# Top-2 expert selection in two token halves, and a first gather table built straight from the token numbers

## The reference

```python
hn = rms_norm(x, norm_ffn[l])
x = x + hier_moe(hn, ...)
# hier_moe, cut
g_idx = jnp.argmax(xt @ w_rg + b_rg, axis=-1)               # 1 group of 4
e_sel = e_logits of that group                              # 8 experts in it
top_v, top_i = lax.top_k(e_sel, 2)                          # 2 experts of the 8
top_w = jax.nn.softmax(top_v, axis=-1) * g_w
h = silu(xt @ w_gate[e]) * (xt @ w_up[e])
out = out + (h * combine[e]) @ w_down[e]
```

## Time and profile before

| | |
|---|---|
| median of 3 runs | 605.76 us (605.17 to 606.72) |
| the profiled execution | 605.26 us, its span 603.5 us |
| PE busy | 577.0 us (96%) |
| DVE busy | 260.3 us (43%) |
| ACT busy | 215.0 us (36%) |
| memory read, written | 147.31 MB, 15.75 MB |
| granted clock of TensorE | 0.999 of 2.4 GHz |

### The profile page before, as it was taken

How to read it: one execution, slowest core, us unless ns; L and a number is a source line. 1 busy time by engine, 2 the same in 40 slices (tenths; PEclk the granted TensorE clock), 3 DMA queues, 4 the chain that set the end, 5 groups by cost and what they waited for, 6 DMA issues and landing times.

```text
span 603.5 us, 8714 instructions
## 1 busy us (share of the span) xinstructions
PE 577.0 (96%) x3442; PEld 437.3 (72%) x3445; DVE 260.3 (43%) x584; ACT 215.0 (36%) x437; POOL 60.3 (10%) x104
## 2 busy tenths in 40 slices
PE   7999999999999999999999998999999999887795
PEld 4978989888788888888888874766666666543452
DVE  4646677645445765533472375212111211103255
ACT  6634566555786522422152241011111111111114
POOL 3110000001000001100000012012211121112001
PEclk9999999999999999999999999999999999999999
DMA  8365130712231222197789677999999999999995
GB/s 296 92 205 177 59 111 5 287 62 71 71 104 46 61 70 71 38 344 280 287 315 406 248 259 273 389 414 423 424 421 423 424 427 419 424 425 424 424 421 208
DMA packets 59291, 155.78 MB, mean 258 GB/s; under 512 B 8284, under 2 KB 38388, under 8 KB 47600
## 3 DMA queue, kind: packets, MB, share of 16 engines
q1 hardware_dynamic: 54512, 145.74, 63.2%
q0 software_dynamic: 4720, 9.45, 4.1%
q10 hardware_dynamic: 16, 0.00, 0.0%
HBM read 147.31 MB, written 15.75 MB: 270 GB/s over the span
## 4 chain that ended last, share of the span: by engine, by line
PE 79%; DMA 11%; DVE 3%; SPq 3%; ACT 1%; issue 1%; POOL 1%; DVEq 0%; POOLq 0%; ACTq 0%
PE mid_rows L810 17%; PE last_rows L810 16%; PE bank L1247 12%; DMA slot2b<-expert_w_up 9%; PE bank L810 7%; PE bank L803 5%; PE mid_rows L1267 5%; SPq L554 3%; PE bank L1321 2%; PE mid_rows L945 2%; PE last_rows L868 2%; PE mid_rows L1340 1%; DMA w<-w_in 1%; PE bank L1347 1%; PE mid_rows L868 1%; PE bank L923 1%
## 5 line engine op out<-in xcount | busy, mean ns | idle before, releaser
L1247 PE MATMUL bank<-slots,xgT 128*64 128x256 f32 x544 | 73.0, 381 | 4.5 <-DMA slot2b<-expert_w_up 1.9
L1910 DVE TENSOR_TENSOR w_low<-w,w_high 128x1024 fp32r<-128x1024 f32 x32 | 39.2, 1225 | 78.6 <-ACT w_high L1524 78.6
L1247 PEld LDWEIGHTS bank<-slots,xgT 128*64 128x64 f32 x544 | 49.2, 137 | 22.2 <-issue 4.0
L1524 ACT ACTIVATE w_high<-w 128x1024 fp32r<-128x1024 f32 x32 | 33.7, 1054 | 48.6 <-PE last_rows L810 48.6
L2265 DVE TENSOR_SCALAR y<-mid_rows,slot_weights 128x512 f32<-128x512 f32 x14 | 10.5, 751 | 88.4 <-PE mid_rows L1267 88.4
L1699 ACT ACTIVATE y<-mid_rows,slot_weights 128x512 f32<-128x512 f32 x14 | 9.6, 687 | 84.5 <-PE mid_rows L1267 56.4
L1247 PE MATMUL bank<-slot2b,xgT 128*64 128x256 f32 x208 | 32.9, 381 | 0.0
L1267 PE MATMUL mid_rows<-slots,hT 128*64 128x512 f32 x112 | 29.1, 594 | 2.7 <-issue 2.7
L1693 ACT ACTIVATE h_silu<-bank 128x256 f32<-128x256 f32 x14 | 5.4, 384 | 66.3 <-PE bank L1247 66.3
L810 PE MATMUL mid_rows<-x_high,w_high 128*128 128x512 f32 x72 | 28.7, 399 | 0.0
L810 PE MATMUL mid_rows<-x_high,w_low 128*128 128x512 f32 x72 | 28.2, 391 | 0.0
(11 more groups left out here) (430 smaller groups left out, 1391.5 us busy)
## 6 DMA issues: line engine op xcount, KB each, us to landing
slots<-expert_w_up SPq DMA_DIRECT2D x18, 1024.0 KB, 23.9
slots<-expert_w_gate SPq DMA_DIRECT2D x17, 1024.0 KB, 12.4
slots<-expert_w_down SPq DMA_DIRECT2D x15, 1024.0 KB, 23.9
slot2b<-expert_w_gate SPq DMA_DIRECT2D x9, 1024.0 KB, 16.9
w<-w_in SPq DMA_DIRECT2D x16, 512.0 KB, 3.6
slot2b<-expert_w_up SPq DMA_DIRECT2D x8, 1024.0 KB, 27.5
slot2a<-expert_w_down SPq DMA_DIRECT2D x6, 1024.0 KB, 21.4
w<-w_in SPq DMA_DIRECT2D x7, 840.0 KB, 4.5
```

The costliest lines, as they stand in the source:

```text
L1247: ins = mm(bank[2][e * SLOTS:(e + 1) * SLOTS, m * FE:(m + 1) * FE], xgT[:, c, e * SLOTS:(e + 1) * SLOTS], weights(own, m, e, c * FE, (c + ...
L1524: A(wh2[:, u % 2, :], raw2[:, u % 2, :], ACT.Copy).then_inc(s["hi_done"], 1)
L1910: V.tensor_tensor(wl2[:, u % 2, :], raw2[:, u % 2, :], wh2[:, u % 2, :].bitcast(F32), ALU.subtract).then_inc(s["lo_done"], 1)
```

## The change

Five things are done together.

1. The selection is cut into functions that take a range of tiles. Tiles 0 and 1 (`lo`) are selected, up to the key of their second choice, before DVE waits for the logits of tiles 2 and 3; tiles 2 and 3 (`hi`) follow, with the last two steps of `lo` between theirs. For this ACT takes two of DVE's four copies of turned tiles, and `token_major(0, 2, 1)` goes between the two halves of the last tile's turn.
2. Pair 0 gets a table of its own. `hot` is compared with the whole number `place` (its constant `first_slots` has the offset of the number in it), and the product has 2 columns, the tokens' numbers. DVE makes column 0 of `gtab` from it, and GpSimd gathers. The old table with its 16 columns is made after that, for pairs 1 to 15.
3. SP issues part 20 only after GpSimd has issued the first gather (`pool_step`).
4. Pair 0's gathered rows are turned into four places in four banks, and copied out in quarters, two by ACT and two by DVE.
5. `keep_busy` counts go from 22, 11, 17 to 14, 5, 8, 5.

```diff
@@ SP
             sp.wait_ge(s["hT_done"], 2 * NT)
+            sp.wait_ge(s["pool_step"], 1)
             load_part(20)
@@ GpSimd
             pool.wait_ge(s["gcolm_done"], 1)
             first_gather(0)
+            pool.sem_inc(s["pool_step"], 1)
             pool.wait_ge(s["xt_done"], 2)
+            pool.wait_ge(s["gcolm_done"], 2)
             first_gather(1)
@@ TensorE
             for k in range(2 * NT):
                 pe.wait_ge(s["hot_done"], k + 1)
+                ins = mm(bank[3][:, TABLE][:, 0:2], hot[:, k, :], by_pair[:, k, 0:2], start=(k == 0),
+                         stop=(k == 2 * NT - 1), skip_group_check=True)
+            ins.then_inc(s["first_done"], 1)
+            keep_busy(8)
+            for k in range(2 * NT):
+                pe.wait_ge(s["hot_done"], 2 * NT + k + 1)
                 ins = mm(bank[3][:, TABLE][:, 0:PAIRS], hot[:, k, :], by_pair[:, k, :], ...)
             ins.then_inc(s["first_done"], 1)
-            keep_busy(17)
+            keep_busy(5)
+            def turn_first():
+                pe.wait_ge(s["gathered0"], 16)
+                xv = xg[0].rearrange("p (q c) -> p c q", c=KC)
+                for c in range(KC):
+                    at = bank[(0, 1, 5, 4)[c // 2]][:, (c % 2 + (2 if c >= 6 else 0)) * P:]
+                    ins = tr(at[:, 0:P], xv[:, c, :])
+                    if c == 1:
+                        ins.then_inc(s["first_done"], 1)
+                    if c % 4 == 3:
+                        ins.then_inc(s["xt_done"], 1)
@@ ScalarE
+            act.wait_ge(s["hT_done"], 4)
+            A(hnT[:, 4:8, P:2 * P], bank[TURNED[1][1]][:, :]..., ACT.Copy).then_inc(s["hnT_outA"], 1)
@@ VectorE
+            g_, e_ = maxima_of(lo)
...
+            l_ = second_key(lo, e_)
+
+            router_out(2, 4, 6)
+            dve.wait_ge(s["rl_out"], 2)
+            g_, e_ = maxima_of(hi)
...
+            for e in range(2):
+                V.tensor_scalar(first_slots[:, e * SLOTS:(e + 1) * SLOTS]..., K["iota"][...]...,
+                                UNIT + e * (SEQ - SLOTS), None, ALU.add)
+            V.tensor_copy(by_pair[:, :, 0:2], bc(K["tokval"], 2))
...
             link(V.tensor_reduce(place[:].rearrange("p (k t) -> p k t", k=2), sel[:], AX, ALU.add))
+            for w in range(2):
+                ks = slice(w * NT, (w + 1) * NT)
+                V.tensor_tensor(hot[:, ks, :], first_slots.unsqueeze(1).to_broadcast([P, NT, P]), bc(place[:, ks], P),
+                                ALU.is_equal).then_inc(s["hot_done"], NT)
...
+            dve.wait_ge(s["first_done"], 1)
+            link(V.tensor_scalar(ztab[:, 0:1], bank[3][:, TABLE][:, 0:1], float(NOWHERE), None, ALU.add))
+            V.tensor_scalar(gtab[:, 0:1], ztab[:, 0:1], 1, None, ALU.logical_shift_right).then_inc(s["gcolm_done"], 1)
```

More of the change, by code:

```diff
@@ L1176, in _ @@
             turn_hn(3)
-            token_major(0, 2, 1)
             route(2, 3)
@@ L1188, in _ @@
                start=False, stop=False, skip_group_check=True)
-            keep_busy(22)
+            keep_busy(14)
             pe.wait_ge(s["selb_done"], 1)
@@ L1241, in gate_or_up @@
                 for c in range(KC):
[L1242 to L1245, removed]
+                    if m == 0 and c % 2 == 0 and halved:
+                        pe.wait_ge(s[("xgt_outA", "xgt_outD")[c // 2 % 2]], c // 4 + 1)
+                    if m == 0 and c == 0 and not halved:
+                        pe.wait_ge(s["xgt_outA"], n + 2)
+                    if m == 0 and c == KC // 2 and not halved:
+                        pe.wait_ge(s["xgt_outD"], n + 2)
                     for e in range(2):
@@ L2172, in _ @@
[L2172 to L2184, removed]
+            def maxima_of(ts):
+                return step(V.tensor_reduce(gmax[:, ts], g_lg[:, ts], AX, ALU.max)), step(V.tensor_reduce(v1[:, ts], e_lg[:, ts], AX, ALU.max))
+            def at_maximum(ts, g_, e_):
+                after(g_)
+                g_ = step(V.tensor_tensor(g_hot[:, ts], g_lg[:, ts], bc(gmax[:, ts], NG), ALU.is_equal))
+                after(e_)
+                return g_, step(V.tensor_tensor(one1[:, ts], e_lg[:, ts], bc(v1[:, ts], NE), ALU.is_equal))
@@ new lines, in keyed, with best_key @@
+            def keyed(ts, g_, e_):
+                after(g_)
+                g_ = step(V.tensor_tensor(g_hot[:, ts], g_hot[:, ts], keys4[:, ts], ALU.mult))
+                after(e_)
+                return g_, step(V.tensor_tensor(one1[:, ts], one1[:, ts], keys8[:, ts], ALU.mult))
+            def best_key(ts, g_, e_):
+                after(g_)
+                g_ = step(V.tensor_reduce(gkey[:, ts], g_hot[:, ts], AX, ALU.max))
+                after(e_)
+                return g_, step(V.tensor_reduce(ekey[:, ts], one1[:, ts], AX, ALU.max))
@@ new lines, in first_choice, with without_first @@
+            def first_choice(ts, g_, e_):
+                after(g_)
+                g_ = step(V.tensor_tensor(g_hot[:, ts], g_hot[:, ts], bc(gkey[:, ts], NG), ALU.is_equal))
+                after(e_)
+                return g_, step(V.tensor_tensor(one1[:, ts], one1[:, ts], bc(ekey[:, ts], NE), ALU.is_equal))
+            def without_first(ts, e_):
+                after(e_)
+                return step(V.scalar_tensor_tensor(out=second[:, ts], in0=one1[:, ts], scalar=-3e38, in1=e_lg[:, ts], op0=ALU.mult,
+                                                   op1=ALU.add))
@@ new lines, in second_maximum, with at_second @@
+            def second_maximum(ts, g_, e_):
+                after(e_)
+                e_ = step(V.tensor_reduce(v2[:, ts], second[:, ts], AX, ALU.max))
+                after(g_)
+                step(V.tensor_tensor(one1[:, ts], one1[:, ts], bc(g_hot[:, ts], NE), ALU.mult))
+                return e_
+            def at_second(ts, e_):
+                after(e_)
+                e_ = step(V.tensor_tensor(one2[:, ts], second[:, ts], bc(v2[:, ts], NE), ALU.is_equal))
+                return e_, step(V.tensor_tensor(gap[:, ts], v2[:, ts], v1[:, ts], ALU.subtract))
@@ new lines, in second_keyed, with second_key, second_choice @@
+            def second_keyed(ts, e_, d_):
+                after(e_)
+                e_ = step(V.tensor_tensor(one2[:, ts], one2[:, ts], keys8[:, ts], ALU.mult))
+                after(d_)
+                return e_, step(V.tensor_tensor(gap[:, ts], gap[:, ts], g_hot[:, ts], ALU.mult))
+            def second_key(ts, e_):
+                after(e_)
+                return step(V.tensor_reduce(ekey[:, ts], one2[:, ts], AX, ALU.max))
+            def second_choice(ts, e_):
+                after(e_)
+                return step(V.tensor_tensor(one2[:, ts], one2[:, ts], bc(ekey[:, ts], NE), ALU.is_equal))
@@ new lines, in second_in_group @@
+            def second_in_group(ts, e_):
+                after(e_)
+                return step(V.tensor_tensor(one2[:, ts], one2[:, ts], bc(g_hot[:, ts], NE), ALU.mult))
+            lo, hi = slice(0, 2), slice(2, 4)
+            g_, e_ = maxima_of(lo)
+            g_, e_ = at_maximum(lo, g_, e_)
+            g_, e_ = keyed(lo, g_, e_)
+            g_, e_ = best_key(lo, g_, e_)
+            g_, e_ = first_choice(lo, g_, e_)
+            e_ = without_first(lo, e_)
+            e_ = second_maximum(lo, g_, e_)
```

97 lines of the change are left out of this document (53 added, 44 removed).

## The result

The change made the kernel slower by 0.2%: 606.54 us against 605.16 us (medians of 20 runs each), ratio 1.0021, interval 1.0014 to 1.0028. That is 1.3 us. The forecast was 1.2 us the other way, 604.5 us.

A forecast was written before the change was run, and what follows sets the result against it. The bound was taken to be the weight stream, which loses 6.7 us before it is full. TensorE gains 1.3 us, the stream 1.2 to 2.2; 605.76 - 1.2 = 604.56, rounded 604.5 us, range 602.9 to 606.6.

The forecast's parts named there:

- What bounds the kernel: Weight stream: full from 392 to 590 us, so only the 6.7 us it loses before then can move the end.
- The tail hangs on the stream: End of the kernel: weights, then rows for the final sum, shift with the stream; no size of its own.
- Selection in halves: DVE's selection of tiles: 0.6 us less, less 0.1 us for later last logits; net gain 0.5 us.
- Table from the whole number: DVE between `place` and `hot`: ten instructions leave the path, gain 1.3 us; the gather would start 1.8 us earlier.
- What the gather meets, part 20: First gather: 0.2 us lost beside DVE's second table, 0.6 us to part 20, issued at 370.4 once GpSimd lets go.
- the term of 0.6 us: First gather: slowed 0.6 us by part 20, which comes when it is past its first half; bounds 0 and 1.8.
- The 0.2 us for DVE's instructions beside the gather: GpSimd's part of the first gather: held 0.2 us by DVE's two `hot` instructions; bounds 0 and 1.3 us.
- `keep_busy`: TensorE's useless products: 14 instead of 21 take 3.1 us, out of the way of an earlier `selb`; no gain counted.
- if TensorE's clock falls in the shorter `keep_busy`: Sign of being wrong: TensorE's clock falls there and the turns get slower; no size given.
- Turning in quarters: Landing of the gather to first gate product: copies run beside the turns, gain 0.3 us, bounds 0 and 0.4.
- TensorE's lead and the sum: Start of pair 0: 1.3 us earlier on TensorE; with the stream's 1.2 to 2.2, a gain of 1.2 us taken.
- Rival C: Gather meets the stream: lands after 8.1 us instead of 3.48, pair 0 2.5 us later; up to 608.3 us; chance 0.10.

The follow-up runs named there:

- before_hold: Kernel before, with part 20 held until GpSimd's issue of the first gather and 27 instead of 17 useless products; 608.74 us, ratio 1.0048 to the kernel before.
- before_fill7: Kernel before, with 7 instead of 17 useless products behind the table; 607.69 us, ratio 1.0039 to the kernel before.
- nohold: Changed kernel without SP's wait for pool_step ahead of part 20; 605.01 us, ratio 0.9993 to the kernel before.
- before_fill22: Kernel before, with 22 instead of 17 useless products behind the table; 605.25 us, ratio 0.9997 to the kernel before.
- fill_all: Changed kernel with all four counts of useless products raised (16, 7, 9, 15 for 14, 5, 8, 5); 604.53 us, ratio 0.9988 to the kernel before.
- fill15: Changed kernel with 15 instead of 5 useless products behind the second table; 605.05 us, ratio 0.9993 to the kernel before.
- no_first_table: nohold_fill_all with pair 0's own table taken out and counts 16, 11 and 23; 604.44 us, ratio 0.9987 to the kernel before.
- late20: Changed kernel with part 20 issued only once the first gather has landed, ahead of part 22; 605.5 us, ratio 1.0005 to the kernel before.
- hold_table2: Changed kernel with part 20 held until the second table's product, and counts 16, 7, 9, 9; 605.14 us, ratio 0.999 to the kernel before.
- nohold_fill_all: The best version: changed kernel without the hold of part 20, counts 16, 7, 9, 11; 603.4 us, ratio 0.9966 to the kernel before.

## Why the prediction was wrong

*What bounds the kernel*: right. The stream's rate over 367 to 390 us goes with the ratios to about 0.2% (before_hold 261 GB/s, the changed kernel 269, before_fill7 271, nohold 294, before 300, before_fill22 302, fill_all 306, fill15 and no_first_table 308, the best 324), but for late20 (306 GB/s) and hold_table2 (326 GB/s): there TensorE's wait for the second gather comes behind, and the stream falls to 419 GB/s in 390 to 480 us, 423 in the best version. That is 0.9 us given back later. What it leaves out is TensorE's clock near the end, which added 1.4 us to the traced execution of before_fill7 and some 2.6 us to that of before_hold; there the chain runs over TensorE's products, not over a transfer. The prediction had no term for it ("The tail hangs on the stream").

*Selection in halves*: right, 0.77 us against 0.6 (3.59 for 4.36). The last logits did not come later, where I had taken 0.1. *Table from the whole number*: from the end of `selb` to the start of `hot` are 1.49 us (363.26 to 364.75), and were 2.94 (364.46 to 367.40); 1.3 us of these 1.45 had been forecast. From `hot` to `gtab` it is 2.26 and was 2.20. So `gtab` came 2.59 us earlier, 0.4 of it not from the change, where 1.8 were forecast.

*What the gather meets, part 20*: the step that failed first. "It goes out at 368.9 + 0.2 + 1.19 + 0.1 = 370.4" had it behind GpSimd's work on the gather; it went out at 367.95, 0.13 us ahead of the start of it. Its data and the gather's therefore ran together from the start, and the term of 0.6 us was 1.9 (5.36 for 3.48). That is the upper bound that I had named, 1.8, taken from the second gather of the earlier trace rows. before_hold shows it by itself: a gather of 5.28 us, a stream later by 1.83 us, and a kernel slower by 0.5%, part of which arises in the tail. The 0.2 us for DVE's instructions beside the gather were nothing: GpSimd's part stayed at 1.20 us, and in late20 the gather was as fast as alone.

*`keep_busy`*: the step that failed worst, since it has no term in the sum at all. I asked whether the fillers stand in the way, and not what they cover. The prediction names the falling clock only among the signs of being wrong ("if TensorE's clock falls in the shorter `keep_busy`"). From the counts it could have been worked out: the old set kept TensorE busy until 1.16 us before the turns, and the new one ends 2.28 us before them. The runs give its price: ten products more in the new kernel win 1.5 to 1.7 us, and ten fewer in the old one cost 2.4 us, 1.04 of them at the head. The Trainium skill, TensorE: Matmul & The Clock Gate, section Why this matters for your kernels, treats idle gaps of TensorE as what takes its clock back to 1.2 GHz. The rows agree in kind (0.50 after the gaps of 2.28 and 3.21 us, 1.00 in fill15 and fill_all, where they were filled). They differ in size: the gaps that the Trainium skill warns of are longer than the 2.28 us here and the 1.20 us in nohold, and the measurement decides.

*Turning in quarters*: right at full clock. From landing to the first gate product it took 1.1 us (372.69 to 373.77 in nohold_fill_all), 1.49 before.

*TensorE's lead and the sum*: "TensorE thus starts pair 0 earlier by 1.8 - 0.2 - 0.6 + 0.3 = 1.3 us". Its first gate product came 0.4 us earlier (375.29 for 375.70) and the half gate 0.5 us later. Rival C had the right sign and the right place, but its price (a gather of 8.1 us) was not what happened; the gather took 1.9 us longer, and the clock did the rest. Undoing one cause gave 0.28% (nohold) or 0.33% (fill_all), both together 0.55%: they add up, as far as the intervals tell.

Open: how much of the clock's fall hangs on each gap. In the trace of nohold it fell behind 1.20 us of standing still, in no_first_table it did not, and in late20 it fell at 366.8 us, where no gap was over 0.6 us and where the changed kernel, fill15 and nohold, in which TensorE runs the same instructions up to there, kept it at 1.00. So it is in part a matter of the execution, and a single trace shows only one outcome. Open too is whether the falls near the end belong to the changes of before_fill7 and before_hold.

## What to carry to other kernels

When a change makes a chain shorter, list every filler and every hold that was sized for the old chain, and give each a term of its own in the sum: what it covered, until when, and what stands there now. A semaphore that an engine counts up behind a transfer says that the transfer was handed over, and not that it was worked on; to keep a load clear of a gather, the gather's landing or a later event has to release it. Where small gathers share the DMA engines with a full stream, look at the next gather as well as the one that is spared. And before a time is put down to the stage that was changed, check how much of it is still there at a mark behind that stage: here the last weight issues split 2.4 us into 1.0 and 1.4.

## What the runs showed of the hardware

A gather of the same size takes 3.5 us alone, 4.3 when it starts with the last load still running, 5.3 when a 1 MB load starts with it, and 8.1 to 8.2 in the full stream. The increment that GpSimd does behind its transfer reached SP before the transfer's own instruction had begun (367.95 and 368.08; 370.41 and 370.54 in before_hold). A small integer instruction on VectorE was held while GpSimd cleared `xg`: 1.00 us instead of 0.16, in no_first_table. And a stretch of lost clock was worth about what it took on the chain: in before_fill7 the stretch from the first gather's landing to the end of pair 0's gate and up products was 1.1 us longer (373.60 to 383.39, was 374.17 to 382.83), and SP's last weight issues were 1.04 us later. The kernel lost 2.4 us since the clock fell a second time, at 564 us, where TensorE was on the chain again.
